# Computing the first product of 28 of 128 dense expert chunks during the choice of experts

## The reference

```python
def one(xb):
    q = (xb @ w_q).reshape(blk, PEER_HEADS, 2, PEER_KDIM // 2)
    s = jnp.einsum('thcd,hcnd->thcn', q, sub_keys).astype(jnp.float32)
    s1, i1 = lax.top_k(s[:, :, 0], PEER_TOPK)
    s2, i2 = lax.top_k(s[:, :, 1], PEER_TOPK)
    cand = (s1[..., :, None] + s2[..., None, :]).reshape(blk, PEER_HEADS, PEER_TOPK * PEER_TOPK)
    sc, ci = lax.top_k(cand, PEER_TOPK)
    e1 = jnp.take_along_axis(i1, ci // PEER_TOPK, axis=-1)
    e2 = jnp.take_along_axis(i2, ci % PEER_TOPK, axis=-1)
    eidx = e1 * N_KEYS + e2
    g = jax.nn.softmax(sc, axis=-1)
    act = jax.nn.gelu(jnp.einsum('td,thkd->thk', xb, u_tab[eidx]).astype(jnp.float32))
    coef = (g * act).astype(xb.dtype)
    return jnp.einsum('thk,thkd->td', coef, v_tab[eidx])
```

## Time and profile before

| | |
|---|---|
| median of 3 runs | 4130.13 us (4129.3 to 4132.23) |
| profiled execution, first to last instruction | 4119.2 us |
| choice of experts, layer 0 | about 764 to 1104 us |
| dense stage, layer 0 | about 1104 to 2300 us |
| choice and dense stage, layer 1 | about 2573 to 2911 and 2911 to 4100 us |
| busy, share of the span | PE 87%, DVE 70%, GpSimd 38%, ScalarE 10% |
| moved by DMA | 1020.8 MB, 248 GB/s over the span |

### The profile page before, as it was taken

The page is one execution under the profiler, slowest core; times in us unless marked ns, Lnnn a source line. Parts: engine busy times, 40 slices in busy tenths (PEclk is TensorE's granted clock), DMA queues, the critical chain, the costliest instruction groups (busy, mean ns, idle before and its releaser), DMA issues.

```text
span 4119.2 us, 49386 instructions
## 1 busy us (share of the span) xinstructions
PE 3582.6 (87%) x15374; PEld 2448.0 (59%) x15374; DVE 2889.6 (70%) x5248; ACT 404.3 (10%) x951; POOL 1575.8 (38%) x1447
## 2 busy tenths in 40 slices
PE   7948895896799999999988899987799999999876
PEld 3612222686666667667655684977566666676543
DVE  3787645399877788877666322699777888877666
ACT  1111111110011100000000100111011000000000
POOL 1446640010055555555544000020255555555543
PEclk9969997995599999999999899975899999999998
DMA  4689873121099999989999427120499999999997
GB/s 147 217 268 326 291 240 97 76 78 38 19 336 333 333 347 353 339 327 357 346 336 348 139 82 118 42 83 26 170 331 336 337 354 337 339 347 342 357 347 276
DMA packets 299029, 1020.82 MB, mean 248 GB/s; under 512 B 57789, under 2 KB 58213, under 8 KB 295726
## 3 DMA queue, kind: packets, MB, share of 16 engines
q0 software_dynamic: 188928, 687.95, 46.5%
q1 hardware_dynamic: 84784, 323.80, 21.2%
q10 hardware_dynamic: 25214, 7.72, 2.1%
HBM read 1013.64 MB, written 5.72 MB: 247 GB/s over the span
## 4 chain that ended last, share of the span: by engine, by line
DVE 31%; PE 30%; DMA 24%; issue 7%; POOL 5%; ACT 1%; SPq 1%; DVEq 0%; POOLq 0%; ACTq 0%
DMA area<-peer_ut_in 7%; DMA area<-peer_v_in,area 6%; PE ps L887 5%; PE ps L878 5%; PE ps L618 4%; POOL area L536 4%; PE ps L630 4%; DVE hn L1667 4%; DVE xs L1667 4%; PE ps L703 3%; DVE area L1659 3%; DMA area<-cache_k_in,area 3%; PE ps L781 3%; DMA hn<-peer_u_in,area 3%; PE ps L819 2%
## 5 line engine op out<-in xcount | busy, mean ns | idle before, releaser
L887 PE MATMUL ps<-area 128*128 128x512 f32 x2048 | 966.2, 616 | 72.1 <-DVE area L1647 72.0
L878 PE MATMUL ps<-hT,area 128*128 128x256 f32 x4096 | 941.8, 384 | 90.5 <-DMA area<-peer_ut_in 90.1
L878 PEld LDWEIGHTS ps<-hT,area 128*128 128x128 f32 x4096 | 775.3, 191 | 341.2 <-issue 246.4
L536 POOL DMA_INDIRECT area<-peer_u_in,area x396 | 471.7, 1191 | 1204.9 <-DVEq L1669 785.9
L536 POOL DMA_INDIRECT area<-peer_v_in,area x396 | 439.5, 1110 | 630.7 <-DVEq L1669 428.7
L887 PEld LDWEIGHTS ps<-area 128*128 128x128 f32 x2048 | 381.3, 195 | 472.5 <-issue 471.3
L819 PEld LDWEIGHTS ps<-area 128*128 128x128 f32 x4096 | 597.7, 228 | 87.1 <-issue 78.3
L819 PE MATMUL ps<-area 128*128 128x32 f32 x4096 | 591.8, 305 | 64.4 <-DVE area L1559 58.6
L1659 DVE CUSTOM_DVE_ANT_0 area<-area,hn 128x1024 f32<-128x1024 f32 x384 | 450.4, 1223 | 112.6 <-DMA area<-peer_u_in,area 61.2
L1667 DVE SCALAR_TENSOR_TENSOR xs<-area,xs 128x1024 f32<-128x1024 f32 x192 | 246.6, 1284 | 202.0 <-DMA area<-peer_v_in,area 126.7
L1552 DVE TENSOR_TENSOR area<-small,area 128x1024 f32<-128x1024 f32 x256 | 312.2, 1220 | 0.8 <-issue 0.5
(11 more groups left out here) (247 smaller groups left out, 3122.6 us busy)
## 6 DMA issues: line engine op xcount, KB each, us to landing
area<-peer_ut_in SPq DMA_DIRECT2D x256, 512.0 KB, 7.5
area<-peer_v_in SPq DMA_DIRECT2D x256, 512.0 KB, 6.2
area<-wq_in SPq DMA_DIRECT2D x8, 2048.0 KB, 19.5
area<-w_in_c_in SPq DMA_DIRECT2D x6, 2048.0 KB, 8.8
area<-w_in_a_in SPq DMA_DIRECT2D x5, 2048.0 KB, 10.3
area<-peer_u_in,area POOLq DMA_INDIRECT x396, 7.0
area<-peer_v_in,area POOLq DMA_INDIRECT x396, 6.6
area<-w_out_a_in SPq DMA_DIRECT2D x2, 2048.0 KB, 10.8
```

The costliest lines, as they stand in the source:

```text
L536: pool.indirect_dma_start(ring[r], None, ins[what + str(l)], bass.IndirectOffsetOnAxis(ap=idx[:, i:i + 1], axis=0)).then_inc(rows_landed[h ...
L878: m = pe.matmul(ps[c % 2][:, 0:DT * P], us[c][:, k, :], hT[:, k, 0:DT * P], start=(k == 0), stop=(k == KD - 1))
L887: m = pe.matmul(ps[2 + 2 * t + h][:, :], cT[:, c % 2, t * P:(t + 1) * P], vs[c % 2][:, h * 512:(h + 1) * 512], start=False, stop=False, sk ...
```

## The change

For the first 28 chunks of each layer the first product and the gelu are made during the choice of experts. PE has a new helper `ahead(count)`; 28 products are made in five places: 8 after queries(2) and ahead of the decoder's second product, 4 after scores(0, q1), 12 between the first 16 gates, 4 after scores(1, q2). ScalarE makes the gelu of each into `acts`, the idle G[1]. The pieces come through two buffers, the decoder's row of `hn` and `gain`; SP waits for `gelu_done` before it loads one again. When all gates of range 0 stand in G[0], DVE multiplies the 28 chunks of it with `acts` in place by one instruction, and PE uses G[0] as the coefficients of 28 second products. The other 100 chunks run as before. The one-hot buffers of the choice move to other places in `area`. Loads of the second table are no longer coupled with those of the first for the first 28 chunks.

```diff
+AHEAD = 28
+UCHUNKS = (NCH - AHEAD) // CB
...
+    acts = G[1][:, 0:AHEAD, :]
+    uahead = [hn[:, TILES, :].rearrange("p (k c) -> p k c", k=KD), gain[:, :].rearrange("p (k c) -> p k c", k=KD)]
...  sync
+            for n in range(AHEAD):
+                if n == 0:
+                    sp.wait_ge(dec_rows_spread, l + 1)
+                elif n == 1:
+                    sp.wait_ge(dots_ready, l * (GT + 1) + 1)
+                else:
+                    sp.wait_ge(gelu_done, l * NCH + n + 1)
+                sp.dma_start(uahead[n % 2], table_u[n * P:(n + 1) * P, :, :]).then_inc(ahead_landed[n % 2], 16)
...
             sp.wait_ge(scores_ready, (l + 1) * (TILES + 1))
-            with sp.Fori(0, NCH // CB) as j:
+            for n in range(2):
+                v_chunk(n * P, n, l * NCH + n + 1)
+            sp.wait_ge(gates_in_psum, l * NCH + CH + 2)
+            for n in range(AHEAD, AHEAD + 2):
+                u_chunk(n * P, n % CB, l * NCH + n + 1)
+            for n in range(2, AHEAD):
+                v_chunk(n * P, n % CB, l * NCH + n + 1)
+            with sp.Fori(0, UCHUNKS - 1) as j:
                 for c in range(CB):
+                    n = AHEAD + c
+                    u_chunk(j * (CB * P) + (n + 2) * P, (c + 2) % CB, j * CB + (l * NCH + n + 3))
+                    v_chunk(j * (CB * P) + n * P, c, j * CB + (l * NCH + n + 1))
...  tensor
+            def ahead(count):
+                for n in range(begun[0], begun[0] + count):
+                    pe.wait_ge(ahead_landed[n % 2], 16 * (l * AHEAD // 2 + n // 2 + 1))
+                    b = abank()
+                    for k in range(KD):
+                        m = pe.matmul(b[:, 0:DT * P], uahead[n % 2][:, k, :], hT[:, k, 0:DT * P],
+                                      start=(k == 0), stop=(k == KD - 1))
+                    m.then_inc(act_bank_full, 1)
+                begun[0] += count
...
             pe.sem_inc(queried, 1)
+            ahead(8)
 
             pe.wait_ge(dec_coefs_ready, l + 1)
...
             scores(0, q1)
+            ahead(4)
             turn(0)
             pe.wait_ge(dve_bank_free, nv[0])
             for n in range(CH // 2):
                 gates(l * NCH + n, n, e2o0, e1o0)
+                if n % 4:
+                    ahead(1)
             scores(1, q2)
+            ahead(4)
             turn(1)
...
-            first(l * NCH, 0)
+            pe.sem_inc(first_done, AHEAD)
+            pe.wait_ge(coefs_ready, l * NCH + AHEAD + 2)
+            def second_ahead(n):
+                pe.wait_ge(v_landed[n % 2], 16 * (l * NCH // 2 + n // 2 + 1))
+                for t in range(DT):
+                    for h in range(2):
+                        m = pe.matmul(ps[2 + 2 * t + h][:, :], G[0][:, n, t * P:(t + 1) * P],
+                                      vs[n % 2][:, h * 512:(h + 1) * 512], start=False, stop=False, skip_group_check=True)
+                m.then_inc(second_done, 1)
+            for n in range(AHEAD):
+                if n == AHEAD - 1:
+                    first(l * NCH + AHEAD, 0)
+                gates(l * NCH + n + CH, n % CB, e2oh, e1oh)
+                second_ahead(n)
...  scalar
+            def ahead(count):
+                for n in range(begun[0], begun[0] + count):
+                    b = take()
+                    step(act.activation(acts[:, n, :], b[:, 0:DT * P], ACT.Gelu_apprx_tanh))
+                    act.sem_inc(act_bank_free, 1)
+                    act.sem_inc(gelu_done, 1)
+                begun[0] += count
...
             queries(1)
+            ahead(8)
             scores(2)
+            ahead(4)
             exps(2, P, PH)
             turn(0)
             for n in range(CH // 2):
                 gates(l * NCH + n, n, G[0], n * OT)
+                if n % 4:
+                    ahead(1)
             scores(3)
+            ahead(4)
             exps(3, P, PH)
             turn(1)
...  vector
+                if r == 0:
+                    dve.wait_ge(gelu_done, l * NCH + AHEAD + 2)
...
+                if r == 0:
+                    step(dve.tensor_tensor(G[0][:, 0:AHEAD, :], G[0][:, 0:AHEAD, :], acts, ALU.mult))
+                    dve.sem_inc(coefs_ready, AHEAD)
+                    with dve.Fori(0, AHEAD // CB) as j:
+                        chunks(j, made=True)
+                    chunks(CH // CB - 1)
```

More of the change, by code:

```diff
@@ L307, in program @@
     pqd = at(35820, 2, PH, DP)
-    e2o0 = [at(8192 + i * OT * P, OT, P) for i in range(2)]
-    e1o0 = [at(10240 + i * OT * CH, OT, CH) for i in range(2)]
+    e2o0 = [at(18432 + i * OT * P, OT, P) for i in range(2)]
+    e1o0 = [at(15360 + i * OT * CH, OT, CH) for i in range(2)]
     eT = at(29000, 3, DT * P)
@@ L405, in program @@
     first_done = sem("first_done")
+    ahead_landed = [sem(f"ahead_landed{i}") for i in range(2)]
     gelu_done = sem("gelu_done")
@@ new lines, in v_chunk @@
+            def v_chunk(first_row, c, used):
+                wait_apart(sp, go, second_done, used)
+                sp.dma_start(vs[c % 2], table_v[bass.ds(first_row, P), :]).then_inc(v_landed[c % 2], 16)
+            sp.wait_ge(scores_ready, (l + 1) * (TILES + 1))
+            for n in range(2):
[3 more added lines that the diff above has]
+                u_chunk(n * P, n % CB, l * NCH + n + 1)
@@ new lines, in tables @@
+            for n in range(2, AHEAD):
+                v_chunk(n * P, n % CB, l * NCH + n + 1)
+            with sp.Fori(0, UCHUNKS - 1) as j:
+                for c in range(CB):
+                    n = AHEAD + c
+                    u_chunk(j * (CB * P) + (n + 2) * P, (c + 2) % CB, j * CB + (l * NCH + n + 3))
+                    v_chunk(j * (CB * P) + n * P, c, j * CB + (l * NCH + n + 1))
+            for n in range(NCH - CB, NCH):
+                if n + 2 < NCH:
+                    u_chunk((n + 2) * P, (n + 2) % CB, l * NCH + n + 3)
+                v_chunk(n * P, n % CB, l * NCH + n + 1)
@@ L821, in gates @@
                 m.then_inc(gates_in_psum, 1)
+            begun = [0]
+            def ahead(count):
[7 more added lines that the diff above has]
+                begun[0] += count
             last_queries()
@@ L904, in chunks @@
                     second(n, c)
-            for r in range(RANGES):
+            chunks(CH // CB - 1, 0)
+            for r in range(1, RANGES):
                 with pe.Fori(0, CH // CB - (r == RANGES - 1)) as j:
@@ L1164, in gelu, with chunks @@
                 act.activation(ga[:, c % 2, :], ps[c % 2][:, 0:DT * P], ACT.Gelu_apprx_tanh).then_inc(gelu_done, 1)
-            for r in range(RANGES):
[L1167 to L1172, removed]
+            act.wait_ge(coefs_ready, l * NCH + AHEAD + 2)
+            with act.Fori(0, AHEAD // CB) as j:
+                for c in range(CB):
+                    gates(j * CB + (l * NCH + CH + c), c, G[1], j * (CB * OT) + c * OT)
+            def chunks(j, r):
+                for c in range(CB):
+                    n = j * CB + (l * NCH + r * CH + c)
+                    gelu(n, c)
+                    if r < RANGES - 1:
+                        gates(n + CH, c, G[(r + 1) % 2], j * (CB * OT) + c * OT)
+            for r in range(RANGES):
+                if r == 0:
+                    chunks(CH // CB - 1, 0)
+                else:
+                    with act.Fori(0, CH // CB) as j:
+                        chunks(j, r)
                 if r % 2 == 0:
@@ L1637, in peer, with chunks @@
                 dve.wait_ge(gates_in_sbuf, l * NCH + (r + 1) * CH + 2)
-                with dve.Fori(0, CH // CB) as j:
+                if r == 0:
+                    dve.wait_ge(gelu_done, l * NCH + AHEAD + 2)
+                def chunks(j, made=False):
                     step.clear()
@@ L1643, in peer @@
                         n = j * CB + (l * NCH + r * CH + c)
[L1645 to L1649, removed]
+                        if not made:
+                            wait_apart(dve, go, gelu_done, n + 3)
+                            wait_apart(dve, go, second_done, n + 1)
+                            dve.tensor_tensor(cT[:, c % 2, :], ga[:, c % 2, :],
+                                              G[r % 2][:, bass.ds(j * CB + c, 1), :].rearrange("p a t -> p (a t)"), ALU.mult)\
+                                .then_inc(coefs_ready, 1)
                         if r < RANGES - 1:
@@ L1671, in peer @@
                         step(dve.tensor_copy(dots[:, bass.ds(j * GBODY, GBODY)], d16[:, :]))
+                if r == 0:
+                    step(dve.tensor_tensor(G[0][:, 0:AHEAD, :], G[0][:, 0:AHEAD, :], acts, ALU.mult))
[3 more added lines that the diff above has]
+                    chunks(CH // CB - 1)
+                else:
+                    with dve.Fori(0, CH // CB) as j:
+                        chunks(j)
                 step.clear()
```

15 lines of the change are left out of this document (7 added, 8 removed).

## The result

The changed kernel takes 4188.1 us (median of 4 runs, 4173.7 to 4196.6) against 4129.7 before: 1.0138 times as long, 95% interval 1.0104 to 1.0172. The profiled execution of after is the fastest of the four, with a span of 4171.8 us, so it shows 52.7 of the loss of 58 us.

A forecast was written before the change was run, and what follows sets the result against it. DMA transfers were taken to pace the dense stage, DVE the choice of experts. Span 4119.2 + 127 (choice) - 82 (dense) - 10 (start) = 4154, plus 10.9 outside = 4165 us; forecast 4140 to 4190, range 4100 to 4220.

The forecast's parts named there:

- The order (a): Choice, tile(2): exps(2) queued behind ahead(8) and ahead(4) makes DVE wait 43.6 us per layer.
- The order (b): Choice, tile(3): twelve products between sixteen gates, then ahead(4), delay the exp DVE wants; 19 us, taken as 20 per layer.
- (c): Choice, tile(4): no products in it, costed at nothing, since gates alone already keep up with DVE.
- The dense stage: 28 chunks per layer at 8.0 us instead of 9.36 and 9.56: gain 82 us in all, bounds 52 to 104.
- the loop of the gathers: Dense stage: dots, release, gathers and landing over two halves, 15.6 to 17.7 us for two chunks, 7.8 to 8.9 each.
- The bound of the sum: Dense stage: 8.7 us a chunk as upper bound, put at a gain of 52 us in place of 82.
- The start of the dense stage: Bank clearing to first second product: ends near 1122 instead of 1128.4; gain 5 us per layer, 10 in all.
- Rival 4: Dense stage: the gathers' loop binds at 8.7 us a chunk, gain 52 in place of 82, 4195 us; chance 0.12.
- Rival 2: Choice: quicker reloads and PE not slowing, delay 2 x 47, gain 92, a draw at 4132 us; chance 0.15.
- Rival 1: Dense stage: DMA at 424 GB/s, chunks at 7.0 us, gain 138, faster at 4109 us; chance 0.13.
- Rival 3: Choice, tile(3): clock stays at 0.5 while gates and products mix, (b) about 100 us, 4325 us; chance 0.07.
- The sign: Slower, 0.85%; hung on DVE's exp waits in the choice, near 43 us in tile(2) and near 20 in tile(3), twice each.

The follow-up runs named there:

- dense_only: The changed kernel without early loads, products and gelus, the 28 chunks multiplied with whatever lies in the buffer: 4073.2 us, 0.987 of before.

## Why the choice got longer: the queue, not the work

**The exp alone moved.** In `exp_first` only ScalarE's order changes.

```diff
             scores(2)
-            ahead(4)
             exps(2, P, PH)
+            ahead(4)
...
             scores(3)
-            ahead(4)
             exps(3, P, PH)
+            ahead(4)
```

> ScalarE alone changes: exps(2) and exps(3) stand directly behind the score copies, ahead of the four early gelus; TensorE keeps its order. Theory (the wait only changes its name: TensorE makes turn(0) and turn(1) behind the same four products, and DVE's first one-hots need them): DVE's wait for the exp falls from 51 us per layer to about 35, a new wait for the turned indices of some 10 us takes its place, and the time falls by 5 to 20 us against the changed kernel. Rival (the place of the exp in ScalarE's queue is the whole cost): the 28 us from the four early gelus go, twice 28, about 4130 us.

Measured: 4162.5 us (4155.2 to 4177.5), 1.0098 of before (1.0059 to 1.0136). DVE's waits in layer 0:

```profile
DVE area L1636 <- ACT area L1183: 26.0, 1, 26.0
DVE area L1645 <- ACTq L1189: 18.1, 2, 10.7
DVE area L1645 <- PE ps L850: 8.8, 6, 2.7
```

The wait for the exp fell by half, the one in tile(3) to nothing, and 18.1 us of a new wait came: DVE's first one-hots want the turned indices (L1189), and TensorE turns them behind the same four products. The 26.0 us of exp that stay are those of the eight products ahead of the decoder's second product: they hold up the scores themselves, and no order on ScalarE helps against that. The choice got shorter by 7.3 and 7.4 us only, 15 in all, inside the theory's 5 to 20. The median is 26 us lower (21 with each kernel taken against before in its own set), which is more than the choice explains; no run shows where the rest lies. The rival, some 4130 us, falls. So one cause has two addresses, the exp on ScalarE and the turn on TensorE.

**The same work in other places.** `spread` makes the same 28 products. The diff is TensorE's; ScalarE has the same order, with each `exps` ahead of its gelus.

```diff
-            ahead(8)
...
             scores(0, q1)
-            ahead(4)
+            ahead(2)
             turn(0)
             pe.wait_ge(dve_bank_free, nv[0])
+            ahead(1)
             for n in range(CH // 2):
                 gates(l * NCH + n, n, e2o0, e1o0)
-                if n % 4:
+                if n % 2:
                     ahead(1)
             scores(1, q2)
-            ahead(4)
+            ahead(3)
             turn(1)
+            ahead(1)
             for n in range(CH // 2, CH):
                 gates(l * NCH + n, n, e2o0, e1o0)
+                if n % 2:
+                    ahead(1)
+            ahead(5)
```

> The same 28 early products per layer, placed only where TensorE idles or waits for DVE: none before the decoder's second product, 2 after scores(0), 1 after turn(0), 8 between the first 16 gates, 3 after scores(1), 1 after turn(1), 8 between the next 16 gates, 5 behind the last gates; on ScalarE each exp stands ahead of the gelus. Theory (the loss is an order of queues, not TensorE's 97 us of work): DVE waits under 10 us per layer in the choice, and the dense gain of 44 us shows: 4130 + 12 - 44, 4075 to 4110 us, faster than both. Rival (TensorE's work or the loads themselves slow the choice down): DVE's waits stay over 20 us per layer, and the time stays over 4130.

Measured: 4085.4 us (4075.4 to 4093.8), 0.9894 of before (0.9859 to 0.9929). TensorE does the same 97 us more, and the choice takes 10.4 and 8.8 us more instead of 61. What is left is mostly the wait for the last gelu (L1208) ahead of the big multiplication. The second row belongs to the first gathers of the dense stage, which the window still covers.

```profile
DVE area L1778 <- ACTq L1208: 7.8, 1, 7.8
DVE area L1763 <- DMA area<-peer_u_in,area: 6.2, 2, 3.4
DVE area L1653 <- PE ps L850: 2.0, 2, 1.8
```

**And three of the last five moved.** `spread2` makes them between the last gates.

```diff
-                if n % 2:
+                if n % 2 or n > CH // 2 + 9:
                     ahead(1)
-            ahead(5)
+            ahead(2)
```

> The version with the products placed in idle time, with three of the last five moved in between the last six gates of tile(4), so that only two stand behind them. In that version DVE still waits 7.8 and 6.3 us for the last gelu before it multiplies the gates. Theory: this wait goes, 10 to 14 us less than the version it comes from, 4065 to 4080 us. Rival (the gates get later by as much, and the exp or the gates' wait takes its place): no difference over 4 us.

Measured: 4066.3 us (4064.5 to 4069.0), 0.9863 of before (0.9847 to 0.988). This beats both kernels, the one before by 1.4% and the changed one by 115 to 122 us (with and without the shift of before between the sets). The theory's time came. Of the 19 us below `spread` (17 against before in each set), the choice gives 6.2 and 3.7, about the lower end of the 10 to 14 that were expected. The wait for the last gelu is gone, and the choice takes 232.4 and 233.5 us. DVE's waits in layer 0's choice, and the whole of it in busy time (905 to 1105 us, columns as in the earlier trace rows), beside that of before:

```profile
DVE area L1704 <- ACT area L1228: 2.9, 1, 2.9
DVE area L1653 <- ACTq L1193: 2.5, 1, 2.5
DVE area L1653 <- PE ps L850: 1.6, 1, 1.6
```
```profile
905.00:1105.00 200.00, 184.97 (x1057) 160.40 (x1054) 191.89 (x586) 36.91 (x79) 11.94 (x9) 0.94 0.29 95
```
```profile
905.00:1104.00 199.00, 139.06 (x615) 124.53 (x614) 194.88 (x602) 20.24 (x47) 11.94 (x9) 0.56 0.10 35
```

The same 200 us hold 185 us of TensorE instead of 139, with DVE at 192 and 195. The clock plays along: with the wide products between the gates the granted clock is 0.94 in this stretch instead of 0.56, and 16 instructions of gates take mostly 1.87 us there, against 3.59 before. (The first wait is of the decoder's gelu and is there before and after.)

## Why the 28 chunks did not get faster than 8.5 us

**Bytes without work.** `bytes_only` is the kernel before without the loads of the first table for chunks 4 to 27; the products are made with old pieces.

```diff
+            for n in range(28):
+                wait_apart(sp, go, first_done, l * NCH + n + 1)
+                if n < 4:
+                    sp.dma_start(us[n % 4], ins[f"peer_ut{l}"][n * P:(n + 1) * P, :, :]).then_inc(u_landed[n % 4], 16)
+                else:
+                    sp.sem_inc(u_landed[n % 4], 16)
...
```

> The kernel before, with the loads of the first table for chunks 4 to 27 of each layer left out (old pieces are used again, so the output isn't the reference's); products, gelus and multiplications stay. It asks whether the bytes or the work of the 28 chunks give the gain. Theory (bytes: the early chunks wait for transfers): the pace falls from 9.35 and 9.56 to TensorE's floor of 8.7 to 8.8 us, nearly the 8.5 to 8.9 of the changed dense stage, and the time is 4130 - 2 x 24 x 0.7 = 4095 us. Rival (the product's work and the chain product, gelu, multiplication set the pace): stays over 9.2 us, 4125 us.

Measured: 4097.2 us (4080.2 to 4114.5), 0.9941 of before (0.9917 to 0.9966). The pace is 8.75 and 8.71. The median is 25 us below before of its set, where 35 were expected.

```profile
1122.00:1358.00 236.00, 234.31 (x1079) 170.83 (x1077) 188.74 (x330) 28.28 (x61) 141.46 (x122) 1.00 0.87 306
```

TensorE is busy 234 of 236 us: it stands at its floor, 8.7 us. So taking away the bytes alone gives the pace of the change; that the change takes 3.45 us of product from each chunk as well bought nothing. Something else holds it at the same level.

**Fewer bytes still.** `no_v` is the changed kernel without the loads of the second table for chunks 2 to 27.

```diff
             for n in range(2, AHEAD):
-                v_chunk(n * P, n % CB, l * NCH + n + 1)
+                wait_apart(sp, go, second_done, l * NCH + n + 1)
+                sp.sem_inc(v_landed[n % 2], 16)
```

> The changed kernel without the loads of the second table for chunks 2 to 27 of each layer (the old pieces are multiplied again, so the output isn't the reference's); all waits and all other work stay. The 28 chunks then move 2.1 MB each instead of 2.6. Theory (a loop of the row gathers sets their pace: dots, issue of four gathers by GpSimd, landing of the last; bandwidth only enters through the landing): the pace goes from 8.5 to about 8.0 us per chunk, the DMA share from 0.86 to about 0.75. Rival (bandwidth at some 300 GB/s sets it): 2.1 MB at 301 GB/s, 7.0 us per chunk, share unchanged.

Measured: 4182.2 us (4179.5 to 4190.7), 1.0151 of before (1.0131 to 1.017).

```profile
1185.00:1410.00 225.00, 180.91 (x626) 111.71 (x625) 170.86 (x290) 10.97 (x27) 139.07 (x114) 0.80 0.73 244
```
```profile
DVE area L1756 <- DMA area<-peer_u_in,area: 33.8, 12, 3.6
```

The pace is 8.62 and 8.60, as in after, with 244 GB/s in place of 301 and the DMA engines at 0.73. Bandwidth is out as the limit here. I had expected 8.0 from shorter landings, and that didn't come: DVE waits for gathered rows all the same (33.8 us, the second row). The table of turns below shows why.

**Shorter dots.** `half_dots` is the changed kernel with DVE's dots of the 28 chunks over half the width; the other half of each row is left out.

```diff
-                                m = dve.tensor_tensor_reduce(row, row, hn[:, t, :], 1.0, 0.0, ALU.mult, ALU.add,
-                                                             d16[:, q:q + 1])
+                                w = D // 2 if made else D
+                                m = dve.tensor_tensor_reduce(row[:, 0:w], row[:, 0:w], hn[:, t, 0:w], 1.0, 0.0,
+                                                             ALU.mult, ALU.add, d16[:, q:q + 1])
```

> The changed kernel with DVE's four dots in the 28 chunks over half the width (the other half of each row is left out, so the output isn't the reference's); gathers and loads are the same. A group of dots takes 2.6 us instead of 4.7. Theory (loop of the gathers over two halves, dots are one link of it): a loop of 17.1 us gets 2.1 us shorter, so 1.05 us less per chunk, about 7.5 us, less what longer landings take back: 7.5 to 8.0. Rival (bandwidth, or TensorE at its low clock): stays at 8.5.

Measured: 4118.3 us (4108.2 to 4135.6), 0.9987 of before (0.9962 to 1.0011). The pace goes to 7.68 and 7.65, and DMA moves more again.

```profile
1185.00:1390.00 205.00, 172.51 (x658) 102.28 (x657) 122.57 (x301) 11.64 (x29) 122.46 (x117) 0.88 0.93 343
```

Here are one turn of the loop in after and one in `half_dots`, from the chain of waits in order of time (start, us, what).

```profile
1229.47 0.76 issue
1230.23 1.23 POOL area L567
1231.46 0.68 issue
1232.15 0.94 POOL area L567
...
1233.39 1.39 POOL area L567
...
1235.08 6.19 DMA area<-peer_u_in,area
...
1241.45 4.68 DVE area L1755 x8
```
```profile
1247.47 0.76 issue
1248.23 1.61 POOL area L567
...
1250.14 0.94 POOL area L567
...
1251.39 0.94 POOL area L567
...
1252.63 6.04 DMA area<-peer_u_in,area
...
1258.84 2.55 DVE area L1756 x8
```

DVE frees a half of the ring, GpSimd issues four gathers one after the other, the last one lands, DVE makes four dots. With two halves, two chunks go per turn. Means over 23 to 27 turns of layer 0, in us (an issue is counted from its start):

| | dots | to first issue | first to fourth issue | fourth issue to next dots | turn |
|---|---|---|---|---|---|
| before | 4.7 | 0.9 | 4.4 | 8.9 | 18.9 |
| after | 4.7 | 1.0 | 4.8 | 7.0 | 17.5 |
| no_v | 4.7 | 1.1 | 5.1 | 6.9 | 17.7 |
| half_dots | 2.5 | 1.1 | 4.6 | 7.2 | 15.4 |

The fourth of these columns is a landing only where DVE stood waiting for the rows; elsewhere DVE was still busy when they came. In after DVE waited in 19 of 23 turns: there the four issues take 5.0 us and the landing 6.9. In `no_v` it waited in 12 of 23, and there the issues take 6.1 and the landing 6.0. (Layer 1: 5.3 and 6.5, against 6.3 and 5.7.) So fewer bytes did shorten the landing, by 0.9 us, and the issues, which now ran beside DVE's dots, took it back. That is why `no_v` has the pace of after.

The dots got 2.1 us shorter, and so did the turn. Half of that, 1.05 us, was expected per chunk; 0.85 and 0.95 came. If DVE's own work had set the pace, a chunk would have got the whole 2.1 us shorter; DVE stood close behind the loop, though, since before half of the dots in `no_v` it did not wait. It is the loop, then, that sets the pace of the 28 chunks after the change, and not bytes, nor TensorE.

## The prediction, step by step

**The order (a), 43.6 us per layer: right.** DVE waited 40.4 and 40.7 us in tile(2). The first eight took 901.84 to 932.95, 31.1 us instead of 33.2: a landing took 3.3 to 4.2 us, median 3.5 (second fence, 900 to 960 us), not the 4.1 of the earlier trace rows. The estimate of 3.2 us from the Trainium skill (DMA: Bandwidth & Descriptors, Anatomy of one DMA) was nearer, 0.3 us off against 0.6 for the row that I kept; the page gives its formula for DMAs issued from GpSimd, and these loads are issued from SP.

```profile
901.84 3.69 PE L862 MATMUL ps<-hT,hn 128*128 128x256 f32 x16 [0.30 <-PE ps L812]
...
909.54 3.72 PE L862 MATMUL ps<-hT,hn 128*128 128x256 f32 x16 [0.56 <-DMA hn<-peer_ut_in]
...
917.16 3.72 PE L862 MATMUL ps<-hT,hn 128*128 128x256 f32 x16 [0.34 <-DMA hn<-peer_ut_in]
...
932.95 10.47 PE L903 MATMUL ps<-area 128*8 128x512 f32 x24
```
```profile
DMA to landing us min/median/max: 3.3/3.5/4.2
```

**The order (b), 20 us: right.** 10.9 us for the exp and 8.8 us in which DVE waited for gates. I had put all of it on the exp. In layer 1 the two are 12.4 and 7.9 us. The clock behaved as assumed: 0.96 in tile(3) with the products, 0.50 in tile(4) with gates alone.

```profile
985.00:1053.00 68.00, 66.66 (x405) 61.16 (x405) 58.30 (x206) 9.44 (x25) 0.00 (x0) 0.96 0.27 86
1080.00:1145.00 65.00, 56.39 (x256) 55.20 (x255) 64.06 (x243) 6.08 (x17) 0.00 (x0) 0.50 0.00 1
```

**(c), tile(4) at nothing: right.** The choice grew by 60.7 and 61.1 us, and waits of 60.1 and 61.0 cover it.

**The dense stage, 82 us: wrong by half.** The failing step is the loop of the gathers. I had it in the sum, at 7.8 to 8.9 us a chunk, and took 8.0 because landing would get shorter with less traffic. It was 8.53 and 8.60 here, and 8.5 to 8.9 in all kernels with this dense stage and full dots. The mechanism was right and two of its terms were too small: the four issues took 4.8 us in place of 3.7, since a gather's issue lasts up to 1.99 us beside DVE's work, and the release took 1.0 in place of 0.6. The landing, which carried the reasoning, was 7.0 at most, near the 6.8 that 8.0 us a chunk leaves for it. The issues could have been read beforehand: in the trace of before they take 4.4 us. The gain per layer up to chunk 27 was 22 and 26 us, not 38 and 44. The bound of the sum is off too: at 8.7 us a chunk the gain is 28 x (0.66 + 0.86) = 43 us, and not 52; 52 belongs to 8.53. Chunks 28 to 31 lost 3 to 4 us in this execution, though in five of the six other kernels with this dense stage they took no longer than before.

**The start of the dense stage, 10 us: half right.** The multiplication took 7.6 us (8.0 were forecast) and lies beside the clearing of the banks. The gain was 3.2 us in layer 0 and 0.1 in layer 1; in layer 1 the first second product of before came 4 us sooner than in layer 0, and I had read layer 0 alone.

```profile
1161.65 7.63 DVE L1770 TENSOR_TENSOR area<-area 128x7168 f32<-128x7168 f32 x1 [0.21 <-DVE area L1721]
```

**The rivals.** Rival 4, the gathers' loop above the 8.0 us of the sum, is what happened; it had 0.12 and was worth more. Its 4195 us beside the 4188 measured says little, as its gain of 52 us came from the slip above: at 8.7 us it would be 4204. Rival 2 wanted a delay of 47 us per layer, and 60 came. Rival 1, chunks at 7.0 us on more bandwidth, is out: 244 GB/s move at the same pace as 301. Rival 3, the low clock in tile(3), didn't come. The sign hung on (a) and (b), and these held.

**How near the time came, and by what luck.** The measured time lies 2 us inside the forecast of 4140 to 4190. The terms that the sum prices did not put it there. They were forecast at 127 - 82 - 10 = +35 us and measured at 121.8 - 43.8 = +78, which is 4208 us. The other 25 us were given back in stretches that the sum held unchanged: 16 in the later dense chunks, 9 outside the choice and the dense stage, neither of them explained. The direction and the delay were foreseen; that the time fell into the forecast was luck.

## What to carry to other kernels

Work that is moved into an idle engine goes into a queue, and what counts is which short instruction stands behind it: here an exp of 0.3 us and a transposition of 0.9 us, for which the busiest engine waits. Place such work behind those instructions, in pieces no longer than the gap that the trace shows; the same 97 us of products per layer cost 61 us in one order and about 5 in the other. When bytes are taken from a stretch, look for a latency loop (free, issue, land, use) just below the present pace, and count it with issue times measured beside the work that will run with them, before the bytes are turned into time.

## What the runs showed of the hardware

A gather's issue on GpSimd takes 0.94 us in some cases and up to 1.99 in others, in the same stretch.

```profile
1235.08 1.99 POOL L567 DMA_INDIRECT area<-peer_u_in,area  x1 [0.31 <-issue]
1238.28 0.94 POOL L567 DMA_INDIRECT area<-peer_u_in,area  x1 [1.21 <-DVEq L1765]
```

(GpSimd timeline of after.) In after, 1185 to 1400 us, 52 of 99 issues are under 1 us; in `half_dots`, 1185 to 1390, it is 66 of 104. What parts them is what DVE was doing when the issue began. If it ran neither a dot nor a product of the one-hots (all of them instructions with two inputs), the issue took 0.94 us: 39 of 39 in after, 37 of 37 in `no_v`, 56 of 56 in `half_dots`. If it ran one, the issue took 1.46 us on average in after (60 cases, 13 of them under 1 us, the longest 1.99). The Trainium skill (SBUF — State Buffer, the section SBUF: two separate sides) says that a GpSimd operation that reads this memory and a VectorE operation with two inputs in it exclude each other for a whole instruction. The figures go the way of that rule; that some issues stayed short beside DVE's work, and whether the lock is the cause, no run here isolates.

The stages of the choice, bound by DVE, repeat within 0.2 us between `before`, `dense_only` and `bytes_only` (228.2 to 228.4 us), while the other 96 chunks, whose work is the same, take between 863 and 887 us. That is as wide as the scatter of the times of one kernel (41 us over 17 runs of before, 27 over 10 of `half_dots`), which may place the scatter in the dense stages; it was not tested apart.
